# Order of copies, waits and low halves in the item loop of a mixer layer, one core

## The reference

```
proj = rms_norm(x) @ w_in          # mq, mk, mv, mo, gates, aq, ak, av
hm = sigmoid(mo) * mlstm_chunkwise(silu(conv(mqk)), mv, i, f)    # 4 heads of 128
q, k = rms_norm(aq), rms_norm(ak)  # 4 heads x 2 halves of 64
p = softmax(mask(q_c @ k_c^T / 8)) # c = 0, 1, chunk-causal
ha = rms_norm((p_0 - lam * p_1) @ av) * 0.8
x = x + concat(rms_norm(hm), ha) @ w_out
```

## Time and profile before

| | |
|---|---|
| three timed runs | 1437.56, 1437.60, 1441.93 us (median 1437.6) |
| profiled execution | 1442.67 us |
| its span | 1440.9 us |
| mean granted TensorE clock | 0.981 |
| PE, DVE, ACT busy | 96%, 69%, 55% of the span |
| item loop | about 124 to 299 us of the span |

### The profile page before, as it was taken

The page is one execution under the profiler, slowest core; times in us unless marked ns, Lnnn a source line. Parts: engine busy times, 40 slices in busy tenths (PEclk is TensorE's granted clock), DMA queues, the critical chain, the costliest instruction groups (busy, mean ns, idle before and its releaser), DMA issues.

```text
span 1440.9 us, 20296 instructions
## 1 busy us (share of the span) xinstructions
PE 1386.9 (96%) x6801; PEld 1087.1 (75%) x6802; DVE 997.1 (69%) x1209; ACT 792.8 (55%) x984; POOL 201.0 (14%) x234
## 2 busy tenths in 40 slices
PE   6998999898999999999999989999999999999998
PEld 6887777675777777777777767766888888888886
DVE  6865565565999999998989978685854224343185
ACT  5445447125799999998988974453244212332121
POOL 2021002010322222221222220051000000000000
PEclk8999999999999999999999999999999999999999
DMA  9111115147899999999999977012313223224131
GB/s 351 60 59 59 59 43 179 61 133 293 318 409 412 411 408 416 416 409 404 414 407 405 410 284 275 1 59 82 123 59 117 80 96 117 73 103 161 64 113 59
DMA packets 60967, 302.57 MB, mean 210 GB/s; under 512 B 9700, under 2 KB 11810, under 8 KB 48108
## 3 DMA queue, kind: packets, MB, share of 16 engines
q1 hardware_dynamic: 49420, 282.15, 49.8%
q10 hardware_dynamic: 6288, 11.44, 2.3%
q0 software_dynamic: 5200, 8.18, 1.7%
HBM read 291.74 MB, written 18.87 MB: 216 GB/s over the span
## 4 chain that ended last, share of the span: by engine, by line
PE 71%; DMA 6%; DVE 4%; issue 3%; ACT 2%; POOL 0%; DVEq 0%; ACTq 0%; SPq 0%; POOLq 0%
PE ps L777 13%; PE ps L1059 12%; PE ps L1044 11%; PE ps L816 7%; DMA ring<-in_w_gate 5%; PE ps L809 4%; PE ps L626 3%; PE ps L1093 3%; PE ps L786 3%; PE ps L877 3%; PE ps L949 2%; PE ps L543 1%; PE ps L494 1%; PE ps L766 1%; PE ps L1003 1%
## 5 line engine op out<-in xcount | busy, mean ns | idle before, releaser
L2231 DVE TENSOR_TENSOR ring_r<-ring,hi 128x2048 fp32r<-128x2048 f32 (+1 forms) x224 | 431.1, 1981 | 23.6 <-ACT hi L1618 21.6
L1618 ACT ACTIVATE hi<-ring 128x2048 fp32r<-128x2048 f32 (+1 forms) x224 | 362.9, 1662 | 13.4 <-DMA ring<-in_w_gate 6.8
L2245 DVE TENSOR_TENSOR ring_r<-ring,ring_two 128x2048 fp32r<-128x2048 f32 (+1 forms) x50 | 103.8, 2107 | 112.2 <-ACT ring_two L1636 112.2
L1636 ACT ACTIVATE ring_two<-ring 128x2048 fp32r<-128x2048 f32 (+1 forms) x46 | 84.0, 1868 | 132.4 <-PE ps L1059 121.6
L777 PE MATMUL ps<-ring_r,XTS 128*128 128x512 f32 x512 | 130.5, 398 | 5.9 <-issue 3.3
L1266 POOL TENSOR_TENSOR rsv<-msv,half 128x1 f32<-128x1 f32 (+2 forms) x32 | 33.2, 1041 | 693.7 <-DVE msv L1804 678.8
L777 PE MATMUL ps<-hi,XTS 128*128 128x512 f32 x512 | 128.8, 394 | 0.0
L1059 PE MATMUL ps<-ring_two,ats 128*128 128x512 f32 x512 | 126.5, 389 | 0.0
L816 PE MATMUL ps<-hi,HIDS 128*64 128x512 f32 x512 | 123.6, 394 | 0.0
L543 PE MATMUL ps<-ring_r,ring_r 128*128 128x512 f32 x448 | 116.6, 410 | 3.8 <-ACT M L1500 3.1
L777 PEld LDWEIGHTS ps<-ring_r,XTS 128*128 128x128 f32 x512 | 98.1, 192 | 29.2 <-issue 6.5
(11 more groups left out here) (365 smaller groups left out, 2235.5 us busy)
## 6 DMA issues: line engine op xcount, KB each, us to landing
ring<-in_w_gate SPq DMA_DIRECT2D x32, 2048.0 KB, 16.0
ring<-in_w_down SPq DMA_DIRECT2D x32, 2048.0 KB, 16.8
ring<-in_w_up SPq DMA_DIRECT2D x32, 2048.0 KB, 18.4
ring<-in_w_ff SPq DMA_DIRECT2D x16, 2048.0 KB, 7.9
ring<-in_w_in SPq DMA_DIRECT2D x9, 2048.0 KB, 9.1
ring<-in_w_out SPq DMA_DIRECT2D x4, 2048.0 KB, 9.4
results<-M SPq DMA_DIRECT2D x4, 1024.0 KB, 16.9
ring<-results SPq DMA_DIRECT2D x8, 512.0 KB, 7.6
```

The lines of the kernel that those rows point to most:

```text
L1618: act.activation(HI[u][:, c], ring[:, s, c], ACT.Copy).then_inc(w_hi, 1)
L1636: act.activation(hi_of(u, a, part_size(u)), raw_of(u, a, part_size(u)), ACT.Copy).then_inc(w2_hi, 1)
L2231: vec.tensor_tensor(ring_r[s][:, c], ring[:, s, c], HI[u][:, c].bitcast(F32), ALU.subtract).then_inc(w_lo, 1)
L2245: ins = vec.tensor_tensor(raw_of(u, a, n, ring_r), raw_of(u, a, n), hi_of(u, a, n).bitcast(F32), ALU.subtract)
```

## The change

Four things are changed.

- ACT, the keys: `normed_out` writes each half of a key tile once, from PSUM (two copies instead of four). A new function `keys_again(i)` copies each half from there, SBUF to SBUF, onto the other half of the partitions, and counts a new semaphore `keys_twice`. It is called after `normed_out` of key tiles 0 and 1 in the projection loop, and at items 3 and 5 for tiles 2 and 3. The scores of a tile's first head on PE wait for it. DVE's `rest_of_turn` waits for two copies of a key tile instead of four.
- ACT, item 1: the copy of the first av piece (`filled_out(0)`) stands ahead of `normed_out` of the last key tile.
- PE, `out_piece`: each pass waits for what it reads. The first waits for the weights' high half, `mixa_hi` and `mixm_hi`; the second for the weights' low half; the third for `mixa_lo` and for the m rows' low half.
- DVE: `lo_1(8, ...)` at items 24 and 25 stands ahead of the decayed rows of the item instead of at the item's end.

```diff
@@ PE, scores
                         pe.wait_ge(turned_lo, TT + i + 1)
+                        pe.wait_ge(keys_twice, 2 * (i + 1))
@@ PE, out_piece
                 if 0 in parts:
                     if t == 0:
                         pe.wait_ge(w1_hi, 2 * j + 2)
-                        pe.wait_ge(w1_lo, 2 * j + 2)
                         pe.wait_ge(mixa_hi, 1)
-                        pe.wait_ge(mixa_lo, 1)
                     if c == 0:
-                        left(pe, ("F", t, "m"))
+                        pe.wait_ge(mixm_hi, t + 1)
                     open_turn(pe, key, bank)
                 for i, (wp, xp) in enumerate(((0, 0), (1, 0), (0, 1))):
+                    if t == 0 and i == 1 and 0 in parts:
+                        pe.wait_ge(w1_lo, 2 * j + 2)
+                    if t == 0 and i == 2 and 1 in parts:
+                        pe.wait_ge(mixa_lo, 1)
+                    if c == 0 and i == 2 and 1 in parts:
+                        left(pe, ("F", t, "m"))
@@ ACT, normed_out
-                    if u == "aq":
-                        parts = [QTWO[c][n][r, :, :]]
-                    else:
-                        parts = [KHH[c][to * QK:(to + 1) * QK, :, n * P:(n + 1) * P] for to in range(2)]
-                    for d in parts:
-                        act.activation(d, q[r, :, :], ACT.Copy, scale=prm[r, gain:gain + 1]).then_inc(turned_hi, 1)
+                    d = QTWO[c][n][r, :, :] if u == "aq" else KHH[c][r, :, n * P:(n + 1) * P]
+                    act.activation(d, q[r, :, :], ACT.Copy, scale=prm[r, gain:gain + 1]).then_inc(turned_hi, 1)
+
+            def keys_again(i):
+                act.wait_ge(turned_hi, 2 * (TT + i + 1))
+                for c in range(2):
+                    r, other, s = slice(c * QK, (c + 1) * QK), slice((1 - c) * QK, (2 - c) * QK), slice(i * P, (i + 1) * P)
+                    act.activation(KHH[c][other, :, s], KHH[c][r, :, s].bitcast(F32), ACT.Copy).then_inc(keys_twice, 1)
@@ ACT, projection loop
                 if k:
                     normed_out(k - 1)
+                if k in (TT + 1, TT + 2):
+                    keys_again(k - TT - 1)
@@ ACT, item loop
                     exps(n)
-                if n == 1:
-                    normed_out(len(NORMED) - 1)
                 if n in (10, 11):
                     hi_1(6, n - 10)
                 if n % 2 and n // 2 < len(FILL_1):
                     filled_out(n // 2)
+                if n == 1:
+                    normed_out(len(NORMED) - 1)
+                if n in (3, 5):
+                    keys_again(TT - 2 + n // 2 - 1)
@@ DVE, rest_of_turn
-                vec.wait_ge(turned_hi, 2 * (k + 1) if u == "aq" else 2 * TT + 4 * (n + 1))
+                vec.wait_ge(turned_hi, 2 * (k + 1))
@@ DVE, item loop
                         wrow_next(n + 1)
+                    if n in (24, 25):
+                        lo_1(8, n - 24)
                     decayed(n)
...
-                if n in (24, 25):
-                    lo_1(8, n - 24)
```

More of the change, by code:

```diff
@@ L292, in build @@
         turned_lo = sem("turned_lo")
+        keys_twice = sem("keys_twice")
         fin_d_sq = sem("fin_d_sq")
```

## The result

| | before | after |
|---|---|---|
| median of the timed runs | 1438.88 us (5 runs, 1437.56 to 1441.93) | 1431.7 us (5 runs, 1429.07 to 1432.1) |
| ratio | | 0.9948, 95% interval 0.9924 to 0.9971 |
| span of the profiled execution | 1440.9 us | 1427.4 us |
| forecast | | 1427.5 us, range 1422.5 to 1433.0 |

The account below looks back on a forecast made before the run. The prediction took PE to bound the kernel, so only its idle stretches and low clock pay. Its terms, -4.0 + 1.2 - 7.3 = -10.1 us off the timed median, gave 1427.5 us, range 1422.5 to 1433.

Parts of the forecast that it names:

- rival B: Leftover PE stalls lower the clock again: one drop gives back up to 2.5 us (1430.0), both 1432.5; chance 0.20.
- hole 2: PE's 3.60 us wait before the second output unit, with waits at neighbouring output pieces; removing them gains 7.3 us.
- forecast as summed: The terms added up without any rival effect: 1427.5 us, own range 1424 to 1430, chance 0.52.
- Rival C: The expert weights' DMA gives or takes time: 1431.9 us, or 1423 with a better phase; chance 0.18.
- hole 1: PE's 2.86 us idle before the projection piece at item 2, and low clock behind: 4.0 us gained despite a new 1.3 stall.
- doubling ahead of the squares: At item 5 two later key copies on ACT delay the squares; PE stalls 1.5 instead of 0.30 us: 1.2 lost.
- items 24 to the twenty transposes: The late output pieces, where ending PE's waits was to gain 7.3 us.
- That holds if 1.3 us of standing still doesn't lower the clock: Condition on the 4.0 us gain at the first items: PE's new stall on DVE's mix leaves the clock at full speed.
- the three stalls: PE's waits before three late output pieces, at 248.70, 261.93 and 274.48: 0.85, 4.06 and 0.6 us gained.
- waits less for DVE's decays: Through item 28 PE waits less for DVE's decayed rows, raising the late gain from 7.05 to 7.5; 7.3 taken.
- D: PE's wait before the second output unit is not for the low halves; only 4.25 us is gained, 1433.3; chance 0.05.
- E: The key doublings' delay on ACT recurs in all 16 first items, costing 14.4 us: 1440.7; chance 0.05.

Follow-up runs that it names:

- start_only: The changed kernel without its edits to the output pieces (PE's waits by pass, the ninth unit's earlier low halves); ratio to the kernel before 0.9996.
- waits_only: The changed kernel with the ninth unit's low halves back at the end of DVE's items 24 and 25, PE's waits by pass kept; ratio to before 0.9972.
- lows_only: The changed kernel with PE's waits back in front of the whole output piece, the low halves still ahead of the decayed rows; ratio to before 0.9960.
- after_again: The changed kernel run and profiled once more with nothing edited; ratio to the kernel before 0.9946.
- end_only: The kernel before with only the output-piece edits: PE's waits by pass and the ninth unit's low halves ahead of the decayed rows; ratio to before 0.9958.
- swap_only_keys_whole: The changed kernel with four key copies from PSUM in one go and no later doubling, projection copy still first; ratio to before 0.9957.

## Why the prediction was right, and where it was off

The time lay in the range and the direction was right. The mechanism of each term was found as described, but the sum was 2.5 too large. Of that, 1.6 is rival B, priced but not taken, and 1.0 is hole 2, sized too large. The measured 1431.7 lies outside the 1424 to 1430 of the forecast as summed; it lies in the stated range because that took in B and C. There is luck in it both ways: in three other executions the clock fell at item 2 as well, which would have cost 1.6 more.

| term | forecast | measured in the two profiles |
|---|---|---|
| hole 1, to the transposes of item 2 | -4.0 | -4.1 (18.79 to 14.68 after the first mark) |
| doubling ahead of the squares, item 6 | +1.2 (0.9 to 1.5) | +1.36 |
| low clock behind it | 0, in rival B | +1.6 |
| items 24 to the twenty transposes | -7.3 | -6.3 (63.78 to 57.46 from the pair at 247.42) |
| stage | -10.1 | -7.57 |

- **Hole 1** was right to 0.1, with the new wait on DVE's mix, because the clock held at item 2. Where it fell there (start_only, waits_only, lows_only) the term is about 2.5.
- **The doubling** was right in place and chain (ACT's squares, DVE's sums, the mix, PE). From the pair's start to the squares' are 1.19, as estimated; the 0.14 more is the gap ahead of it, 0.61 behind the projection copy's start where the squares had 0.47. The estimate by the Trainium skill's figures (VectorE: DVE Perf Modes, the section on the TRN2 errata), 613 ns a copy and so 1.23 for two, lies between these 1.19 and the 1.28 that the pair's row shows.
- **Failed: "That holds if 1.3 us of standing still doesn't lower the clock"** and the same for the 1.5 at item 6. Rival B had 0.20. Five executions have both leftover stalls (after, after_again, start_only, waits_only, lows_only): the clock fell three times of five behind the first and four times of five behind the second, and none of the five had neither. By these five it should have been the likeliest case. In the five executions whose stall at item 6 is 0.30 or 0.31 it never fell there. Its price was off the other way, 1.6 a fall, not 2.5: the 5.49 against 2.99 of the earlier trace rows was a stretch of 6.83 us at 0.50, and every fall behind a leftover stall of the changed kernel lasted 3.41. The length of the hole does not decide between the two: end_only has the same 2.86 and 3.41 us of low clock.
- **Hole 2**: the three stalls gave 0.77, 4.05 and 0.61, as forecast (0.85, 4.06, 0.6), and no new one came. The size was off by what a piece takes once it starts while the pair ahead of it is still running (0.41 behind the start of a pair that lasts 0.86): 2.95 from start to start at item 24 against 2.81 before, 3.06 at item 26 against the 2.85 that I used, 3.17 at item 28 (266.72 to 269.89) against 2.84. The trace of before had this already, at item 25: 253.10 to 256.17, 3.07. It is not the waits inside the pieces, since lows_only has none and takes 3.07 at item 26 (255.72 to 258.79). The added 0.25 for "waits less for DVE's decays" did not come.
- **The base**: three runs gave 1437.6; with five the kernel before is at 1438.9, and at 1438.0 and 1438.5 in the larger sets. About 1 of the 4.2 us between 1427.5 and 1431.7 is that.
- **Rival C** is real in size (the expert stage spreads by 5.4) but goes with no edit: as far as the runs show it is spread within each kernel's runs, not a shift. D and E are out: hole 2's wait was the low halves' (waits_only names it, DVE L1859), and from item 7 on PE stood 0.45, 0.25 and 0.55, as before.

## What to carry to other kernels

Work that is split to shorten a wait must be put where its engine is idle, not merely later: the same two copies cost 2.9 us ahead of a square (1.3 of stall, 1.6 of low clock) and nothing two instructions further on. A stall that shrinks from 2.9 to 1.2 us is not priced by its length alone; ask whether the clock holds, and if it may not, spend the effort on making the stall vanish. Where single runs spread by more than the edit is worth, compare one stage between two marks in the profile, read the clock in it before two kernels are compared, and say which differences lie outside it.

## What the runs showed of the hardware

- PE's clock fell to the 1.2 GHz level behind stalls of 1.2 to 1.6 us, in some executions and not in others of the same code up to there. Behind the same 2.86 us hole twelve matmuls took 5.49 in one execution (before) and 4.57 in another (end_only).
- In the ten profiles the clock stood at 0.50 in fourteen stretches between 118 and 320 us: twelve lasted 3.41 us, and two 6.83 (item 2 of before and of swap_only_keys_whole). A short one cost about 1.6 us of matmul time, the long one of swap_only_keys_whole 2.8.
- A fall needs no marked stall: in waits_only and lows_only the clock was also at 0.50 from about 314.5 us on, with PE 100% busy, behind 32 matmuls of 36 columns; eight transposes then took 1.84 us (waits_only) against 1.07 at the full clock (start_only).
- A piece of twelve 128x512 matmuls that starts on an idle PE takes 2.81 to 2.84 us from start to start, and 2.95 to 3.17 when it starts while the pair of 128x384 or 128x512 ahead is still running: part of a removed stall comes back there.
- A copy of 64x512 from SBUF to SBUF on ACT is no dearer than one from PSUM with a gain: pairs of 1.28 and 1.39 us.
